# Strassen's seven block products for fourteen of sixteen units of the second feed-forward matrix, with the weight sums on GpSimd

## The reference, cut to what matters

```python
h = layer_norm_2(ALPHA * h + mix, ln1_g, ln1_b)            # 256 x 1024
up = jnp.square(jax.nn.relu(h @ w_ff1))                    # w_ff1: 1024 x 4096
h = layer_norm_2(ALPHA * h + up @ w_ff2, ln2_g, ln2_b)     # w_ff2: 4096 x 1024
```

## Time and profile before

| | us |
|---|---|
| median of 3 runs | 1676.76 |
| lowest and highest run | 1674.03, 1676.86 |
| the profiled execution, first to last instruction | 1675.9 |
| TensorE, VectorE, ScalarE, GpSimd busy | 1635.3, 890.5, 721.8, 32.6 |
| mean granted TensorE clock | 0.991 of full speed |

### The profile page before, as it was taken

One profiled execution on the slowest core, in us unless ns is written; L12 is line 12 of the kernel. 1 busy time (PEld: TensorE's weight loads), 2 busy tenths in 40 slices (PEclk: granted clock), 3 DMA queues, 4 the chain that ended last, 5 costly groups with the idle time before them and its releaser, 6 DMA issues.

```text
span 1675.9 us, 25227 instructions
## 1 busy us (share of the span) xinstructions
PE 1635.3 (98%) x10724; PEld 1285.9 (77%) x10724; DVE 890.5 (53%) x1190; ACT 721.8 (43%) x1084; POOL 32.6 (2%) x56
## 2 busy tenths in 40 slices
PE   8999999998999999997999999999999999999998
PEld 7878644435988644434989998989989899988997
DVE  7777421104677411104658656655566676575555
ACT  4775211112675211113655544544456564444443
POOL 0000000000000000000000000000000000000000
PEclk9999999998999999998999999999999999999999
DMA  9637999997837999997745565555556455555552
GB/s 270 230 126 283 353 416 418 416 417 255 269 134 271 357 416 418 417 417 273 218 136 175 176 202 176 193 184 185 192 157 199 134 169 177 201 192 185 185 192 76
DMA packets 193109, 413.07 MB, mean 246 GB/s; under 512 B 16416, under 2 KB 130848, under 8 KB 176608
## 3 DMA queue, kind: packets, MB, share of 16 engines
q1 hardware_dynamic: 191904, 409.81, 68.3%
q10 hardware_dynamic: 1088, 1.57, 0.4%
HBM read 409.52 MB, written 1.84 MB: 245 GB/s over the span
## 4 chain that ended last, share of the span: by engine, by line
PE 90%; DVE 3%; DMA 3%; ACT 2%; issue 1%; SPq 1%; POOL 0%; ACTq 0%; DVEq 0%
PE PS L1700 13%; PE PS L513 11%; PE PS L517 11%; PE PS L514 11%; PE PS L521 9%; PE PS L525 9%; PE PS L524 9%; PE PS L1723 5%; DMA weights_raw<-in_w_in 3%; PE PS L540 2%; PE PS L1676 2%; PE PS L1732 2%; DVE hT_lo L729 1%; DVE weights_low L493 1%; ACT arena L863 0%
## 5 line engine op out<-in xcount | busy, mean ns | idle before, releaser
L493 DVE TENSOR_TENSOR weights_low<-weights_raw,weights_hi 128x1024 fp32r<-128x1024 f32 x368 | 431.2, 1216 | 199.7 <-ACT weights_hi L488 198.8
L488 ACT ACTIVATE weights_hi<-weights_raw 128x1024 fp32r<-128x1024 f32 x368 | 365.7, 1046 | 136.6 <-PE PS L525 66.6
L513 PE MATMUL PS<-hT_hi,weights_hi 128*128 128x256 f32 (+1 forms) x1456 | 411.4, 283 | 0.9 <-ACT bias L955 0.9
L517 PE MATMUL PS<-hT_hi,weights_low 128*128 128x256 f32 (+1 forms) x1456 | 409.6, 281 | 1.4 <-DVE weights_low L493 1.4
L514 PE MATMUL PS<-hT_lo,weights_hi 128*128 128x256 f32 (+1 forms) x1456 | 409.2, 281 | 0.0
L513 PEld LDWEIGHTS PS<-hT_hi,weights_hi 128*128 128x128 f32 (+1 forms) x1456 | 274.6, 189 | 4.8 <-issue 2.7
L517 PEld LDWEIGHTS PS<-hT_hi,weights_low 128*128 128x128 f32 (+1 forms) x1456 | 274.8, 189 | 2.0 <-DVE weights_low L493 1.8
L514 PEld LDWEIGHTS PS<-hT_lo,weights_hi 128*128 128x128 f32 (+1 forms) x1456 | 274.8, 189 | 1.2
L525 PE MATMUL PS<-weights_hi,opa_lo 128*128 128x512 f32 x384 | 152.6, 397 | 0.0
L521 PE MATMUL PS<-weights_hi,opa_hi 128*128 128x512 f32 x384 | 152.4, 397 | 0.2
L524 PE MATMUL PS<-weights_low,opa_hi 128*128 128x512 f32 x384 | 151.0, 393 | 0.0
(11 more groups left out here) (335 smaller groups left out, 2367.7 us busy)
## 6 DMA issues: line engine op xcount, KB each, us to landing
weights_raw<-in_w_in SPq DMA_DIRECT2D x80, 1024.0 KB, 5.5
weights_raw<-in_w_ff SPq DMA_DIRECT2D x64, 1024.0 KB, 5.2
arena<-in_w_down SPq DMA_DIRECT2D x22, 1024.0 KB, 22.8
arena<-in_w_gate SPq DMA_DIRECT2D x20, 1024.0 KB, 15.0
weights_raw<-in_w_up SPq DMA_DIRECT2D x20, 1024.0 KB, 17.3
weights_raw<-in_w_gate SPq DMA_DIRECT2D x20, 1024.0 KB, 17.6
arena<-in_w_up SPq DMA_DIRECT2D x16, 1024.0 KB, 13.7
weights_raw<-in_w_down SPq DMA_DIRECT2D x16, 1024.0 KB, 16.0
```

The source lines that it names most:

```text
L488: act.activation(u.flat[0][:, c:e], u.x[:, c:e], ACT.Copy).then_inc(*sig.mark("w_hi", u.u, i))
L493: dve.tensor_tensor(u.flat[1][:, c:e], u.x[:, c:e], u.flat[0][:, c:e].bitcast(F32), ALU.subtract).then_inc(*sig.mark("w_lo", u.u, i))
L513: pe.matmul(o, w[0], x[0], start=start, stop=False)
L517: return pe.matmul(o, w[1], x[0], start=False, stop=stop)
```

## The change

A block product of 2 x 2 blocks takes seven products in place of eight (Strassen's scheme, in Winograd's form). Units `ff2 0` to `ff2 13` of each layer are done in this way; `ff2 14` and `ff2 15` stay as they were. A unit is seen as four blocks of 128 x 512 (two of rows, two of columns), the squared activations as four of 128 x 128.

- VectorE forms, beside the square, four combinations of the activation blocks (three dependent ops of 256, 128 and 128 columns); high and low parts are then made of seven blocks, 896 columns, in place of 512.
- GpSimd forms four sums of weight blocks, each of 128 x 512 with two inputs (`unit_sums`), from the loaded unit into memory in the arena, two places by turns; the sums of unit i wait for `ff2 i-2`. Three raw blocks and four sums are split: ScalarE's high parts have 2048 + 1536 columns, VectorE's low parts as many, in place of 2048.
- On ScalarE the sums' high parts follow the factors' high part and come ahead of those of the unit's raw blocks. On VectorE the low parts of a unit are made in its own stage, behind those of the factors (`sums_vector`), and no longer by `feed`.
- TensorE does seven products, 21 matmuls, for a unit (`seven_products`), into seven banks that accumulate over the 14 units. `ff1` has one bank left, bank 0, for all its stages.
- After stage 13 ScalarE copies four of the banks to memory, and VectorE puts the seven together with ALPHA·h (`combine`, 11 ops of 512 columns) ahead of the last norm. The last two units start their banks anew.

The two halves of the `ff1` tile swap places so that the blocks lie in order; that and the places in memory are left out here.

```diff
...
@@ -425,6 +426,17 @@
+SEVEN = 4 * D // 256 - 2
+N_FACTOR = 7
+factors = [unit_own[:, 0, 1024 * i:1024 * i + 1024].rearrange("p (f s) -> p f s", f=8) for i in range(2)]
...
+sums_at = (2048, 4096), (9216, 11264)
...
+def factor_slot(part, i):
+    n = N_FACTOR * P
+    return opa_flat[part][:, n * (i % 2):n * (i % 2) + n].rearrange("p (f s) -> p f s", f=N_FACTOR)
...
@@ -437,6 +449,12 @@
+        self.seven = self.name.startswith("ff2 ") and int(self.name.split()[1]) < SEVEN
+        if self.seven:
+            i = int(self.name.split()[1])
+            low, hi = (s[i % 2] for s in sums_at)
+            self.pieces = (0, 512), (1024, 2048)
+            self.sums = mem(low, UNIT), arena_hi[:, hi:hi + UNIT], arena_hi[:, low:low + UNIT]
@@ -484,10 +502,49 @@
-    for i, (c, e) in enumerate(u.halves):
+    for i, (c, e) in enumerate(u.pieces if u.seven else u.halves):
+def sums_scalar(act, name):
+    u = units[place[name]]
+    for i in range(2):
+        act.wait_ge(*sig.at("unit_sums", name, i))
+        act.activation(u.sums[1][:, 1024 * i:1024 * i + 1024], u.sums[0][:, 1024 * i:1024 * i + 1024], ACT.Copy).then_inc(
+            *sig.mark("w_hi", u.u, 2 + i))
+def sums_vector(dve, name):
+    u = units[place[name]]
+    dve.wait_ge(*sig.at("unit_sums", name, 1))
+    for i, (c, e) in enumerate(u.pieces):
+        dve.wait_ge(*sig.at("w_hi", u.u, i))
+        dve.tensor_tensor(u.flat[1][:, c:e], u.x[:, c:e], u.flat[0][:, c:e].bitcast(F32),
+                          ALU.subtract).then_inc(*sig.mark("w_lo", u.u, i))
+    for i in range(2):
+        c, e = 1024 * i, 1024 * i + 1024
+        dve.wait_ge(*sig.at("w_hi", u.u, 2 + i))
+        dve.tensor_tensor(u.sums[2][:, c:e], u.sums[0][:, c:e], u.sums[1][:, c:e].bitcast(F32),
+                          ALU.subtract).then_inc(*sig.mark("w_lo", u.u, 2 + i))
+def unit_sums(pool, name):
+    u = units[place[name]]
+    i, l = int(name.split()[1]), name.split()[2]
+    x = u.x.rearrange("p (b n) -> p b n", b=4)
+    s = u.sums[0].rearrange("p (b n) -> p b n", b=4)
+    if i > 1:
+        pool.wait_ge(*sig.at("ps", f"ff2 {i - 2} {l}"))
+    pool.wait_ge(*sig.at(f"raw{u.raw}_loaded", u.u))
+    pool.tensor_tensor(s[:, 0, :], x[:, 0, :], x[:, 1, :], ALU.add).then_inc(*sig.mark("unit_sums", name, "first"))
+    pool.tensor_tensor(s[:, 1, :], x[:, 1, :], x[:, 3, :], ALU.add).then_inc(*sig.mark("unit_sums", name, 0))
+    pool.wait_ge(*sig.at("unit_sums", name, "first"))
+    pool.tensor_tensor(s[:, 2, :], s[:, 0, :], x[:, 3, :], ALU.add).then_inc(*sig.mark("unit_sums", name, "third"))
+    pool.wait_ge(*sig.at("unit_sums", name, "third"))
+    pool.tensor_tensor(s[:, 3, :], s[:, 2, :], x[:, 2, :], ALU.add).then_inc(*sig.mark("unit_sums", name, 1))
 def split_vector(dve, u):
+    if u.seven:
+        return
...
@@ -636,6 +694,33 @@
+SEVEN_BANKS = 5, 1, 4, 6, 2, 7, 3
+def seven_products(pe, name, l):
+    u, i = units[place[name]], int(name.split()[1])
+    if i == 0:
+        for q, b in enumerate(SEVEN_BANKS):
+            banks.hold(pe, f"seven {q} {l}", (b,), "act_took" if b > 3 else "dve_took")
+    hi, lo = factor_slot(0, i), factor_slot(1, i)
+    raw_block = lambda b: tuple(v[:, 512 * b:512 * b + 512] for v in u.flat)
+    sum_block = lambda b: tuple(v[:, 512 * b:512 * b + 512] for v in u.sums[1:])
+    made = -1
+    for q, f, w, ready in ((0, 5, raw_block(0), 0), (1, 4, raw_block(2), 1), (4, 3, raw_block(3), 1),
+                           (3, 1, sum_block(0), 2), (5, 0, sum_block(1), 2),
+                           (2, 2, sum_block(2), 3), (6, 6, sum_block(3), 3)):
+        o = PS[:, SEVEN_BANKS[q], :]
+        if ready > made:
+            pe.wait_ge(*sig.at("w_hi", u.u, ready))
+        pe.matmul(o, hi[:, f, :], w[0], start=i == 0, stop=False)
+        pe.matmul(o, lo[:, f, :], w[0], start=False, stop=False)
+        if ready > made:
+            pe.wait_ge(*sig.at("w_lo", u.u, ready))
+            made = ready
+        last = pe.matmul(o, hi[:, f, :], w[1], start=False, stop=i == SEVEN - 1)
+    last.then_inc(*sig.mark("ps", name))
...
@@ -2258,17 +2343,18 @@
...
-            project_T(pe, L(f"ff1 {i + 1}"), hT, "act_took", among=4, between=turn_first() if i == 0 else None)
-        if i < N_STAGE - 2:
+            project_T(pe, L(f"ff1 {i + 1}"), hT, "act_took", among=1, between=turn_first() if i == 0 else None,
...
+        if i < SEVEN:
-            accumulate_rows(pe, L(f"ff2 {i}"), opa, 2 * (i % 4), n_("ln2b"), i == 0, False)
-    accumulate_rows(pe, L(f"ff2 {N_STAGE - 2}", f"ff2 {N_STAGE - 1}"), opa, 4, n_("ln2b"), False, True,
+            seven_products(pe, n_(f"ff2 {i}"), l)
+    accumulate_rows(pe, L(f"ff2 {N_STAGE - 2}", f"ff2 {N_STAGE - 1}"), opa, 0, n_("ln2b"), True, True,
@@ -2402,10 +2488,22 @@
-            if i > 3:
-                act.wait_ge(*sig.at("ps", n_(f"ff2 {i - 4}")))
-            q = 2 * (i % 4)
-            hi_part(act, opa[0][:, q:q + 2, :], relu2[i % 2]).then_inc(*sig.mark("ff_act", n_(f"up {i}")))
+            if 1 < i <= SEVEN:
+                act.wait_ge(*sig.at("ps", n_(f"ff2 {i - 2}")))
+            elif i > SEVEN:
+                act.wait_ge(*sig.at("ps", n_(f"ff2 {SEVEN - 1}")))
+            if i < SEVEN:
+                hi_part(act, factor_slot(0, i), factors[i % 2][:, 0:N_FACTOR, :]).then_inc(
+                    *sig.mark("ff_act", n_(f"up {i}")))
+                sums_scalar(act, n_(f"ff2 {i}"))
+            else:
+                q = 2 * (i - SEVEN)
+                hi_part(act, opa[0][:, q:q + 2, :], relu2[i % 2]).then_inc(*sig.mark("ff_act", n_(f"up {i}")))
+            if i == SEVEN:
+                act.wait_ge(*sig.at("ps", n_(f"ff2 {SEVEN - 1}")))
+                for b in range(4):
+                    q = SEVEN_BANKS.index(4 + b)
+                    copy(from_banks[:, b, :], PS[:, 4 + b, :]).then_inc(*sig.mark("act_took", f"seven {q} {l}"))
@@ -2414,6 +2512,27 @@
 def vector_block2(dve, feed, l):
+    def combine(l):
+        c = "seven_dve"
+        part = {SEVEN_BANKS.index(4 + b): from_banks[:, b, :] for b in range(4)}
+        bank = {q: PS[:, SEVEN_BANKS[q], :] for q in (1, 4, 6)}
+        rest = [[h[:, t, 512 * n:512 * n + 512] for n in range(2)] for t in range(NT)]
+        for q in part:
+            dve.wait_ge(*sig.at("act_took", f"seven {q} {l}"))
+        step(dve, c, dve.tensor_tensor(part[2], part[2], part[0], ALU.subtract))
+        dve.scalar_tensor_tensor(rest[0][0], rest[0][0], ALPHA, part[0], ALU.mult, ALU.add).then_inc(*sig.mark(c))
+        step(dve, c, dve.tensor_tensor(part[3], part[2], part[3], ALU.subtract))
+        dve.tensor_tensor(rest[0][0], rest[0][0], bank[1], ALU.add).then_inc(*sig.mark("dve_took", f"seven 1 {l}"))
+        dve.scalar_tensor_tensor(rest[0][1], rest[0][1], ALPHA, part[3], ALU.mult, ALU.add).then_inc(*sig.mark(c))
+        dve.scalar_tensor_tensor(rest[1][1], rest[1][1], ALPHA, part[3], ALU.mult, ALU.add).then_inc(*sig.mark(c))
+        step(dve, c, dve.scalar_tensor_tensor(rest[1][0], rest[1][0], ALPHA, part[2], ALU.mult, ALU.subtract))
+        dve.tensor_tensor(rest[0][1], rest[0][1], bank[4], ALU.subtract).then_inc(*sig.mark("dve_took", f"seven 4 {l}"))
+        dve.tensor_tensor(rest[1][1], rest[1][1], part[5], ALU.subtract).then_inc(*sig.mark(c))
+        step(dve, c, dve.tensor_tensor(rest[1][0], rest[1][0], part[5], ALU.add))
+        step(dve, "dve_took", dve.tensor_tensor(rest[1][0], rest[1][0], bank[6], ALU.add), f"seven 6 {l}")
@@ -2586,15 +2705,29 @@
-            dve.tensor_tensor(relu2[i % 2], relu_t[i % 2], relu_t[i % 2], ALU.mult).then_inc(
-                *sig.mark("ff_dve", n_(f"square {i}")))
-            q = 2 * (i % 4)
-            dve.wait_ge(*sig.at("ff_act", n_(f"up {i}")))
-            lo_part(dve, opa[1][:, q:q + 2, :], relu2[i % 2], opa[0][:, q:q + 2, :]).then_inc(
-                *sig.mark("ff_dve", n_(f"up {i}")))
+            if i < SEVEN:
+                f = factors[i % 2]
+                r = relu_t[i % 2].rearrange("p c (t s) -> p c t s", t=NT)
+                step(dve, "ff_dve", dve.tensor_tensor(f[:, 4:8, :].rearrange("p (t c) s -> p c t s", t=NT), r, r, ALU.mult))
+                step(dve, "ff_dve", dve.tensor_tensor(f[:, 0:2, :], f[:, 5:7, :], bcast_mid(f[:, 7, :], 2), ALU.subtract))
+                step(dve, "ff_dve", dve.tensor_tensor(f[:, 2, :], f[:, 1, :], f[:, 5, :], ALU.add))
+                dve.tensor_tensor(f[:, 3, :], f[:, 2, :], f[:, 4, :], ALU.subtract).then_inc(
+                    *sig.mark("ff_dve", n_(f"square {i}")))
+                dve.wait_ge(*sig.at("ff_act", n_(f"up {i}")))
+                lo_part(dve, factor_slot(1, i), f[:, 0:N_FACTOR, :], factor_slot(0, i)).then_inc(
+                    *sig.mark("ff_dve", n_(f"up {i}")))
+                sums_vector(dve, n_(f"ff2 {i}"))
+            else:
+                dve.tensor_tensor(relu2[i % 2], relu_t[i % 2], relu_t[i % 2], ALU.mult).then_inc(
+                    *sig.mark("ff_dve", n_(f"square {i}")))
+                q = 2 * (i - SEVEN)
```

(29 more changed lines are left out.)

2 lines of the change are left out of this document (added).

## The result

The changed kernel took 1794.94 us (median of 4 runs, 1791.40 to 1800.38) against 1676.19 (median of 4, 1674.03 to 1676.86): a ratio of 1.0717 with a 95% interval of 1.0696 to 1.0738. The forecast of 1808 was 13 us high, and its range of 1720 to 1880 held the result.

What follows compares the result with a forecast made beforehand. The prediction took TensorE, busy 98% of the span, to bound the kernel before. With L = 15.4, 26 L - 269 gave +131 us over both layers; on 1676.8 that made 1808 us, range 1720 to 1880.

Steps and rivals of the forecast that it cites:

- The loop of 11.9 without collisions: One feed-forward stage of VectorE and ScalarE waiting on each other: 11.9 us before any GpSimd collision.
- A sum costs 0.97 us: VectorE's loss per colliding GpSimd sum: a length of 1.12 us less 0.15 of overlapped start-up.
- Four collisions less 0.4: Per stage, four GpSimd sums delay VectorE 3.9 us, less 0.4 for handovers they fall into: 3.5 us.
- L = 15.4: L is the time of one feed-forward stage's VectorE and ScalarE loop, collisions included: 15.4 us.
- Thirteen equal loops: In each layer, 13 loops of L each lead from H of stage 0 to H of stage 13.
- H of stage 13: H is the end of ScalarE's high part of a stage's factors, from which loops are counted; here stage 13's.
- 2 us for the early sums: Sums made ahead of stage 0 meet the splits there: 2 us added over both layers.
- TensorE's wait before a unit: TensorE idle 4 to 5 us in each stage, released by VectorE's low parts.
- The ends of 34.8 and 32.5: From H of stage 13 to tile 1's sum: 34.8 us in layer 0, 32.5 in the other.
- the first (sums beside VectorE, 1717): Rival: GpSimd's sums run beside VectorE without collision, L = 11.9, +40 us, 1717 us; chance 13%.
- The second (TensorE sets the pace, 1671): Rival: VectorE's loop falls under TensorE's 10.59 us a stage; gain 19.6, ends cost 14, 1671 us; chance 7%.
- The third (the clock, 1889): Rival: TensorE's clock drops after its wait before each ff2 unit, L = 18.5, +212 us, 1889 us; chance 8%.

Runs made afterwards that it cites:

- e1: The changed kernel without GpSimd's four sums a unit, h being split in their place: 1709.25 us, ratio 1.0207.
- e3: The changed kernel without GpSimd's sums (h split in their place) and with raw blocks rounded and split ahead of the factors: 1671.23 us, ratio 0.9974.
- e4b: The kernel before the change with four unused GpSimd adds of 128x512 in each of stages 0 to 13: 1685.62 us, ratio 1.0061.
- e11: e3 with the 11 ops of `combine` left out too: 1660.81 us, ratio 0.9913.
- e7: The changed kernel with raw blocks ahead of the factors and the four sums on VectorE instead of GpSimd: 1699.02 us, ratio 1.0147.

## Why the prediction was right, and where it wasn't

The sign, the place, the mechanism and roughly the size hold. The profiled executions differ by 114.3 us (1790.2 and 1675.9); the forecast said 131. These rows of VectorE after, the loops' ends and tile 1's sums, carry the account (the first square of layer 1 is at 1559.57):

```profile
1056.39 0.69 DVE L2711 TENSOR_TENSOR units_of_experts<-arena 128x512 f32<-128x512 f32 x1 [4.01 <-ACT arena L2488]
1066.50 0.68 DVE L2711 TENSOR_TENSOR units_of_experts<-arena 128x512 f32<-128x512 f32 x1
1247.51 0.68 DVE L2711 TENSOR_TENSOR units_of_experts<-arena 128x512 f32<-128x512 f32 x1
1284.97 1.22 DVE L844 SCALAR_TENSOR_TENSOR h<-h,PS 128x1024 f32<-128x1024 f32 x1
1748.21 0.69 DVE L2711 TENSOR_TENSOR units_of_experts<-arena 128x512 f32<-128x512 f32 x1
1783.05 1.21 DVE L844 SCALAR_TENSOR_TENSOR h<-h,PS 128x1024 f32<-128x1024 f32 x1
```

- **The loop of 11.9 without collisions: right.** e1 gives 11.87, e3 shows that the order causes it.
- **A sum costs 0.97 us: right, by two errors that cancel.** An undisturbed sum takes 1.28 us, not 1.12, and 0.30 of its start is overlapped, not 0.15: the 128-column op grew from 0.29 to 1.27, so 0.98. The overlap had been read from one select that met a subtraction half way.
- **Four collisions less 0.4: nearly.** A stage with four is 11.87 + 3 x 0.98 + 1.08 = 15.89 us (measured 15.92 to 15.94), one with three 14.81 (14.78 and 14.79). But only ten of the 24 middle loops have four, eight have three, and six take 13.56 to 13.82: how many of the four ops the sums catch depends on when ff2 i-2 ends, and the forecast took all four for every stage. The mean of the twelve middle loops is 181.01 / 12 = 15.08 in layer 0 and 178.53 / 12 = 14.88 in layer 1, against L = 15.4: -3.8 and -6.3 us.
- **Thirteen equal loops: wrong for the first.** The step "13 loops to H of stage 13" counted the first of a layer like the others. It takes 10.11 us (1056.39 to 1066.50): the raw blocks of unit 0 had been rounded and sums 0 and 1 made before it. That is -5.3 a layer, -10.6 together, and the largest miss.
- **2 us for the early sums: wrong, 7.8.** From the norm's last writes to the first square it is 13.25 and 14.80 us (1043.14 to 1056.39, 1544.77 to 1559.57) where it was 10.12 and 10.13: +3.1 and +4.7. Eight sums meet the norm and two low parts, as e4b shows by itself.
- **TensorE's wait before a unit: there, but shorter, and its releaser wrong.** Forecast were 4 to 5 us in each stage, released by VectorE's low parts. The largest row of TensorE's waits (us in total, times, longest) has 20 waits of 3.6 us at most, released by ScalarE's high part of the raw piece:

```profile
PE PS L717 <- ACT weights_hi L506: 56.4, 20, 3.6
```

- **The ends of 34.8 and 32.5: right.** From the square of stage 13 to tile 1's sum 2.8 + 34.8 and 2.8 + 32.5 us were forecast, and 37.46 and 34.84 measured, and `combine` 7.2 in place of 7.5.

The rest of the two programs differs by -1.4 (114.3 less 7.8 at the starts and less 56.5 and 51.4 from first square to tile 1's sum). So 131.1 - 10.6 - 10.1 - 0.6 + 5.8 - 1.4 = 114.2, for the 114.3 measured. That the forecast came within 13 us of 1795 owes something to luck: the price of a sum is two errors that cancel, and the starts make up for part of what the loops were overrated.

Of the rivals, the first (sums beside VectorE, 1717) described e1's kernel, which came to 1709; in the changed kernel the sums do collide. The second (TensorE sets the pace, 1671) is e3 to the microsecond, but e3 makes no sums; with the change's order and its sums it can't be had. The third (the clock, 1889) had the row right and the consequence wrong; its sum was wrong too, since half of the 4.9 us on top of 15.4 is 17.9 and not 18.5, and so about 1872. The granted clock does fall to the lower level after such a wait as the 3.55 us above, and the matmuls do come 0.43 us apart, but the unit still ends in the shade of VectorE's loop: the stages are within 0.1 us of 11.87 plus what their collisions cost, with no term for the clock. Its one trace is the end of the unit, which sets when the sums begin, and where it came late the stage was the shorter for it.

Where the expected 19.6 us went can be read off the runs. Without sums and recombination 14.9 of them are there (e11, 1660.8 against 1675.7); `combine` takes back 10.4 (e3); making the sums on VectorE costs 28 more (e7), or as the change has them, on GpSimd in the first order, 124.
